# Conv inputs and the out projection's operand turned in 32 x 32 blocks on VectorE and re-partitioned through DRAM, in place of TensorE transposes

## The chip, the cores and the metric

One NeuronCore of one Trainium2 chip. The metric is the device time of one launch in microseconds (us); the kernel before takes 1271.84 us, the median of 3 runs (1271.75 to 1272.41). All numbers of the trace come from one profiled execution of the kernel before.

## The reference

Two decoder layers over x (256 tokens, 2048 channels), all float32. Each layer projects x with one wide matrix, runs three causal mixers on the result, and sends the concatenated mixer outputs through an output projection, a residual and a layer norm.

```python
(aq, ak, av, ag, su, sv, sg, mq, mk, mv, mo, mg, mi, mf) = split_columns(x @ w_in)
# A: three dilated window attentions, merged by their softmax denominators -> att
# B: sgu = u * (causal 128x128 mixing of the layer-normed v)
# C: mLSTM in chunks of 128; its q and k first pass a causal depthwise convolution of width 4
qk = silu(causal_depthwise_conv(concat(mq, mk), conv_w, conv_b))      # 2048 channels
h  = mlstm_chunkwise(q, k, v, ig, lf) * sigmoid(mo)
ml = head_norm(h, head_norm_g)
mix = concat([att * silu(ag), sgu * silu(sg), ml * silu(mg)])          # 256 x 2048
x  = layer_norm(alpha * x + mix @ w_out)
```

## The kernel before

The tokens are two tiles of 128 (`TT = 2`), the model's 2048 channels are 16 tiles of 128 (`KT`). A projection of 512 columns is a block: 8 chunks (`CH`) of 256 weight rows each. There are 23 blocks of `w_in` and 4 of `w_out` in a layer. Each float32 product is made of three passes in the fp32r type: the operand and the weights are both split into a high part and the rest (hi and lo), and hi x hi, hi x lo and lo x hi are summed in PSUM. So a chunk is 12 matmuls of 512 columns (`chunks`, L373): 2 row tiles, 2 token tiles, 3 passes.

The weights flow through a ring of four: SP issues a 512 KB load into `w_raw[c % 4]` (L324) when VectorE has finished with that slot; ScalarE copies it to `w_hi` (L736) as soon as TensorE has left the slot of `w_hi` of four chunks ago; VectorE subtracts to get `w_lo` (L1060); TensorE uses both. Everything else on ScalarE and VectorE is written between these splits in a fixed order, as is the order on SP. Each engine and each queue works strictly in its written order.

The operand of a matmul needs channels on the partitions. Where a projection's result (tokens on the partitions) becomes an operand or must be scanned along the tokens, TensorE transposes it:

- the convolution: 4 blocks of 512 columns, mq and mk (`N_CONV` to `N_CONV + 3`). Each is copied out of PSUM to `z[:, i % 2]` by ScalarE (tile 0) and VectorE (tile 1) in the next block's fourth chunk (`take`), transposed by 8 matmuls with the identity (L639, in `conv_transposes`), and then ScalarE makes bias + last tap from PSUM (L961), VectorE adds three taps, 12 instructions for 512 channels (L1404), and ScalarE applies SiLU into `qkT` (L967).
- the out projection's operand, `mix`: 8 units of 2 channel tiles, 4 transposes each (L391, in `transposes`), then the hi copy on ScalarE (L755) and the lo part on VectorE (L1084). The first two units stand inside block `N_SG`, the rest between the chunks of the first `w_out` block (`first_block`).

The blocks at the end of a layer, in the order of TensorE: `N_CONV` .. `N_CONV + 3`, `N_MV` and `N_MV + 1` (values of the mLSTM), `N_MG1` (second half of its gate), `N_SG` (gate of B), `N_OUT` .. `N_OUT + 3`. The mLSTM's score matmuls (L671) stand after the first chunks of `N_MV + 1` and wait for all of the convolution (`conv_silu`). The value matmuls (L690 to L692) stand in the block behind it. VectorE turns them into h, statistics and the normed h (`head_output`, L1462); GpSimd multiplies by the gain and by the gate (L1732, L1737). The lines of two helpers recur in the rows: L1137 and L1133 are 32 x 32 block transposes of VectorE that the attention part uses already.

## Time and profile before

| | |
|---|---|
| median of 3 runs | 1271.84 us (1271.75 to 1272.41) |
| span of the profiled execution, first to last instruction | 1269.9 us |
| TensorE busy | 1257.0 us, 99% |
| VectorE busy | 893.0 us, 70% |
| ScalarE busy | 705.4 us, 56% |
| GpSimd busy | 244.0 us, 19% |
| mean granted TensorE clock | 0.997 of full speed |
| DMA, mean | 209 GB/s, 264.97 MB |

The profiled execution's own time is not listed apart from its span; the median of the runs stands 1.9 us above the span. Matmuls overlap, so the duration of one (some 390 ns) is longer than its spacing (some 227 ns); the spacing is read from the chain of waits, where the pieces follow each other. "Idle before, releaser" says how long an engine stood still before an instruction, and whose end let it go.

### The profile page before, as it was taken

To read this page: it belongs to the slowest core of one execution; us is meant where nothing else is said; L and a number is where in the kernel's file an instruction comes from. 1 tells how busy PE (TensorE), PEld (TensorE's weight loads), DVE (VectorE), ACT (ScalarE), POOL (GpSimd) and SP (SyncE) were. 2 spreads that over 40 slices of the span, in tenths; PEclk is the share of its full clock that TensorE was granted. 3 is DMA by queue.
4 is the path that set the end of the run, shared out by engine and by line. 5 is a ranking of instruction groups with operands and counts; after the bars stand their busy time and mean duration, and the time that the engine had idled before them with its cause. 6 is when DMAs were issued, how large, how long until landed. Compare 5 with 4: busy or idle time off the path is not lost.

```text
span 1269.9 us, 16388 instructions
## 1 busy us (share of the span) xinstructions
PE 1257.0 (99%) x6342; PEld 1040.2 (82%) x6342; DVE 893.0 (70%) x1229; ACT 705.4 (56%) x989; POOL 244.0 (19%) x268
## 2 busy tenths in 40 slices
PE   9999999999999999999999999999999999999996
PEld 8888888878888888888888788888888888888885
DVE  5686876876667655865785779768665776567656
ACT  5477476575555544444563775666755555345441
POOL 0321522522220000400003223334131200004000
PEclk9999999999999999999999999999999999999998
DMA  9968768765665555465657587678546556565562
GB/s 336 310 209 261 236 189 277 260 192 164 204 195 174 184 186 185 152 230 190 207 186 238 183 282 245 193 258 282 184 149 215 183 157 209 165 197 198 186 212 86
DMA packets 129277, 264.97 MB, mean 209 GB/s; under 512 B 8824, under 2 KB 8976, under 8 KB 128688
## 3 DMA queue, kind: packets, MB, share of 16 engines
q1 hardware_dynamic: 123712, 247.23, 60.6%
q0 software_dynamic: 3680, 13.28, 3.0%
q10 hardware_dynamic: 1808, 3.42, 0.7%
q8 instruction: 50, 0.82, 0.3%
q14 instruction: 27, 0.22, 0.0%
HBM read 258.61 MB, written 5.28 MB: 208 GB/s over the span
## 4 chain that ended last, share of the span: by engine, by line
PE 86%; ACT 4%; DVE 4%; POOL 3%; issue 2%; DVEq 0%; POOLq 0%; ACTq 0%
PE ps L373 79%; ACT arena L810 2%; DVE w_lo L1060 2%; ACT w_hi L736 2%; PE ps L444 1%; PE ps L671 1%; PE ps L391 1%; PE ps L639 1%; POOL arena L1684 1%; PE ps L533 0%; POOL arena L1680 0%; PE ps L518 0%; ACT arena L807 0%; PE ps L355 0%; DVE arena L1133 0%
## 5 line engine op out<-in xcount | busy, mean ns | idle before, releaser
L1060 DVE TENSOR_TENSOR w_lo<-w_raw,w_hi 128x1024 fp32r<-128x1024 f32 x408 | 527.1, 1305 | 326.4 <-ACT w_hi L736 324.5
L736 ACT ACTIVATE w_hi<-w_raw 128x1024 fp32r<-128x1024 f32 x408 | 427.3, 1058 | 388.9 <-PE ps L373 339.3
L373 PE MATMUL ps<-w_hi,xT_hi 128*128 128x512 f32 x1616 | 636.2, 394 | 0.7 <-DVE w_lo L1060 0.7
L373 PE MATMUL ps<-w_hi,xT_lo 128*128 128x512 f32 x1616 | 629.6, 390 | 0.0
L373 PE MATMUL ps<-w_lo,xT_hi 128*128 128x512 f32 x1616 | 629.0, 389 | 0.0
L373 PEld LDWEIGHTS ps<-w_hi,xT_hi 128*128 128x128 f32 x1616 | 303.4, 188 | 64.3 <-issue 1.3
L373 PEld LDWEIGHTS ps<-w_hi,xT_lo 128*128 128x128 f32 x1616 | 303.3, 188 | 64.0
L373 PEld LDWEIGHTS ps<-w_lo,xT_hi 128*128 128x128 f32 x1616 | 303.6, 188 | 61.4
L292 POOL TENSOR_TENSOR carried<-ident 1x1 f32<-1x1 f32 x30 | 19.6, 652 | 454.8 <-DVE arena L1416 178.7
L1217 DVE CUSTOM_DVE_ANT_0 mix<-xres,mix 128x1024 f32<-128x1024 f32 x64 | 89.0, 1390 | 1.1
L807 ACT ACTIVATE arena<-arena 32x256 f32<-32x256 f32 x128 | 53.2, 416 | 15.6 <-DVE arena L1137 14.0
L373 PE MATMUL ps<-ahead,xT_hi 128*128 128x512 f32 x160 | 49.8, 392 | 0.0
L1630 POOL TENSOR_TENSOR su<-z,sincos 128x128 f32<-128x128 f32 x24 | 23.6, 1005 | 122.0 <-ACT z L796 100.9
L1404 DVE SCALAR_TENSOR_TENSOR conv_y<-ps,cw,conv_y 128x255 f32<-128x255 f32 (+2 forms) x96 | 41.7, 476 | 1.1
L1060 DVE TENSOR_TENSOR ahead<-w_raw,ahead 128x1024 fp32r<-128x1024 f32 x23 | 27.5, 1223 | 15.1 <-ACT ahead L736 15.0
L736 ACT ACTIVATE ahead<-w_raw 128x1024 fp32r<-128x1024 f32 x23 | 23.8, 1056 | 22.8 <-DMA w_raw<-w_out_dram 7.2
L373 PEld LDWEIGHTS ps<-ahead,xT_hi 128*128 128x128 f32 x160 | 29.7, 188 | 5.9
L373 PE MATMUL ps<-ahead,xT_lo 128*128 128x512 f32 x80 | 31.2, 390 | 0.0
L810 ACT ACTIVATE arena<-arena 32x256 f32<-32x256 f32 x64 | 26.6, 416 | 7.3 <-DVE arena L1133 6.5
L825 ACT ACTIVATE arena<-arena 32x256 f32<-32x256 f32 x64 | 26.6, 415 | 6.8 <-DVE arena L1165 5.9
L967 ACT ACTIVATE arena<-conv_y 128x512 f32<-128x512 f32 x16 | 10.1, 633 | 32.7 <-DVE conv_y L1404 32.7
L1732 POOL TENSOR_TENSOR store<-store,hg 128x1024 f32<-128x1024 f32 x4 | 11.4, 2876 | 76.5 <-DVE store L1462 76.5
(244 smaller groups left out, 825.3 us busy)
## 6 DMA issues: line engine op xcount, KB each, us to landing
w_raw<-w_in_dram SPq DMA_DIRECT2D x367, 512.0 KB, 4.5
w_raw<-w_out_dram SPq DMA_DIRECT2D x64, 512.0 KB, 4.8
mix<-gate_w_dram SPq DMA_DIRECT2D x32, 512.0 KB, 5.6
xres<-x_dram ACTq DMA_DIRECT2D x4, 512.0 KB, 8.4
v_dram<-arena POOLq DMA_DIRECT2D x4, 512.0 KB, 6.3
z<-v_dram POOLq DMA_DIRECT2D x8, 256.0 KB, 5.6
z<-ln_g_dram POOLq DMA_DIRECT2D x2, 1024.0 KB, 7.7
store<-ln_b_dram POOLq DMA_DIRECT2D x2, 1024.0 KB, 7.9
```

The costliest lines, as they stand in the source:

```text
L292: nc.gpsimd.tensor_tensor(carried[0:1, at:at + 1], ident[0:1, 0:1], ident[0:1, 0:1], ALU.mult)
L373: mm = pe.matmul(ps[2 * s + t][:], a[:, order[c] * KC + k, t * P:(t + 1) * P], b[:, k], start=(c + k + i == 0), stop=(c == CH - 1 and k == ...
L391: tr = pe.transpose(ps[4 + u % 4][:, (k * TT + t) * P:(k * TT + t + 1) * P], src[:, t, at * P:(at + 1) * P], ident[:])
L444: mm = pe.matmul(ps[t][:], a[:, c * KC + k, t * P:(t + 1) * P], b[:, k], start=False, stop=(c == CH - 1 and k == KC - 1 and i == 2))
L736: A(hi_of(n, c), w_raw[:, c % RING], ACT.Copy).then_inc(w_hi_done, 1)
L807: mv_ = A(dst.rearrange("p m (r t u i) -> p u t (m r) i", r=RES, t=TT, u=4)[:, u], src.rearrange("p (t f q i) -> p f t q i", t=TT, f=4, i= ...
L810: mv_ = A(dst.rearrange("p m (t u s) -> p u t m s", t=TT, u=4)[:, u], src.rearrange("p (t m f s) -> p f t m s", t=TT, m=PAIRS, f=4)[:, f], ...
L825: e = A(pTC[f * 32:(f + 1) * 32, :, u * 32:(u + 1) * 32], zp[u * 32:(u + 1) * 32].rearrange("p (s f i) -> p f s i", s=SLOTS, f=4)[:, f], A ...
L1060: TTn(lo_of(n, c), w_raw[:, c % RING], hi_of(n, c).bitcast(F32), ALU.subtract).then_inc(w_lo_done, 1)
L1217: f = V.tensor_tensor_reduce(gate_junk, xres[:, tt, half * KH:(half + 1) * KH], gate_rows[buf], 1.0, 0.0, ALU.mult, ALU.add, gate_acc[:, t ...
L1404: f = STT(y, ps[4 + hf][:, t * SEQ:(t + 1) * SEQ - back], cw[:, m, j:j + 1], y, ALU.mult, ALU.add)
L1630: G.tensor_tensor(rope_a[:, :, :, c], v[:, :, :, c], trig(1), ALU.mult)
```

## The change

Neither transposes of TensorE (L639, L391) remain; those of the attention part, the gates and the next layer's x stay.

- **Convolution.** VectorE turns the 128 x 1024 tile of a block in 32 x 32 blocks (one STREAM_TRANSPOSE). That leaves each 32-token, 32-channel square transposed in place, so channels still have to move between partition quadrants: SP stores the turned tile to DRAM (`put_conv`, one DMA, rows of 576 bytes) and reads it back in four DMAs of 32 partitions each (`fetch_conv`). A halo of 3 tokens is filled by a memset and a small copy. Bias and taps then read the SBUF tile `conv_T` where they read PSUM before.
- **Out projection's operand.** `mix` goes the same way in four parts of 512 channels (`put`, `fetch`, rows of 512 bytes): ATT, ML_A, SGU, ML_B. The hi and lo instructions are now 128 x 1024 for ATT, SGU and ML_A, and two of 128 x 512 for ML_B.
- **Order.** The last two `w_in` blocks change places (gate of B first, then the second half of the mLSTM's gate). VectorE takes over the product of gate and gained h for ML_A and ML_B; GpSimd multiplies by the gain in halves (before: all of h, then all of the gate). The loads of the final layer norm's gain and bias on GpSimd's queue move behind the store and fetch of ML_B. The weights of `w_out` are read in plain order.

The diff, cut to its core:

```diff
+                def put_conv(i):
+                    sp.wait_ge(conv_turned, l * 4 + i + 1)
+                    dst = conv_dram[l, i].rearrange("f t u j x -> (u j) (f t) x")
+                    src = conv_zT.rearrange("p f (t m) x -> p (f t) (m x)", t=TT)
+                    sp.dma_start(dst, src).then_inc(conv_put, 16)
+                def fetch_conv(i):
+                    sp.wait_ge(conv_put, (l * 4 + i + 1) * 16)
+                    ...
+                    for f in range(4):
+                        sp.dma_start(dst[f * QUARTER:(f + 1) * QUARTER], src[f]).then_inc(conv_moved, 16)
...
+                        if c == 1 and N_CONV + 2 <= n <= N_CONV + 5:
+                            fetch_conv(n - N_CONV - 2)
+                        if c == CH - 1 and N_CONV + 1 <= n <= N_CONV + 4:
+                            put_conv(n - N_CONV - 1)
...
+                load(w_in, N_MG1, (MG + 1) * BW, plain, puts={0: ATT, 6: ML_A, 7: SGU}, fetches={2: ATT})
+                load(w_out, N_OUT, 0, plain, puts={7: ML_B}, fetches={0: ML_A, 1: SGU})
+                load(w_out, N_OUT + 1, BW, plain, fetches={0: ML_B})
...
@@ TensorE @@
-                    chunks(N_CONV + i, Q_CONV + i, i % 2, 0, 2)
-                    conv_transposes(i - 1)
-                    chunks(N_CONV + i, Q_CONV + i, i % 2, 2, 6)
+                    chunks(N_CONV + i, Q_CONV + i, i % 2, 0, 6)
...
-                transposes(mix, CH, OUT_ORDER, 0, ((h_done, (l + 1) * MH), (mix_att, l + 1)))
-                transposes(mix, CH, OUT_ORDER, 1)
-                chunks(N_SG, Q_SG, 1, 4, CH)
-                first_block(N_OUT, Q_OUT, mix, CH, OUT_ORDER, 2, {
-                    2: ((h_done, (l + 1) * MH), (mix_ml, l + 1)),
-                    6: ((z_dve, taken_dve(l, Q_SG)),)})
+                chunks(N_MG1, Q_MG1, 1, 0, CH)
+                for c in range(CH):
+                    pe.wait_ge(mixT_lo, step(l, c))
+                    chunks(N_OUT, Q_OUT, 0, c, c + 1)
...
@@ ScalarE, convolution @@
-                    act.wait_ge(conv_ps, l * 4 + i + 1)
+                    split(n + 1, 0, 2)
+                    act.wait_ge(conv_moved, (l * 4 + i + 1) * 4 * 16)
...
@@ VectorE, convolution @@
+                    take(n, i % 2, z[:, i % 2, 1, :])
+                    V.transpose(conv_zT.rearrange("p f b x -> p b f x")[:, :, :, HALO:],
+                                z[:, i % 2].rearrange("p t c -> p (t c)")).then_inc(conv_turned, 1)
+                    split(n, 4, 6)
...
+                    split(n, 6, 8)
+                    split(n + 1, 0, 2)
+                    dve.wait_ge(conv_moved, (l * 4 + i + 1) * 4 * 16)
+                    V.memset(conv_T[:, 0, :, 1:HALO], 0.0)
+                    own(V.tensor_copy(conv_T[:, 1:, :, 1:HALO], conv_T[:, :-1, :, QUARTER + 1:]))
...
+                        split(n + 1, 2 + hf, 3 + hf)
...
@@ VectorE, from the normed h to the out projection @@
+                own(TTn(mix[:, :, 2 * BW:3 * BW], mix[:, :, 2 * BW:3 * BW], store[:, 1], ALU.mult))
+                turn_mix(ML_A)
+                split(N_MG1, 3, 4)
+                TTn(mix[:, :, BW:2 * BW], mix[:, :, BW:2 * BW], su[:], ALU.mult).then_inc(z_dve, 1)
+                turn_mix(SGU)
+                split(N_MG1, 4, 8)
+                operand(ATT, 0)
+                split(N_OUT, 0, 4)
+                TTn(mix[:, :, 3 * BW:4 * BW], mix[:, :, 3 * BW:4 * BW], store[:, 2], ALU.mult).then_inc(z_dve, 1)
+                turn_mix(ML_B)
+                operand(SGU, 1)
+                operand(ML_A, 2)
+                split(N_OUT, 4, 8)
+                operand(ML_B, 3, 0, KC)
+                operand(ML_B, 4, KC, KC)
```

How the change moves instructions, first on SP. This is its queue from the convolution to the end of the first layer, before: nothing but weight loads (L324).

```order
L324 DMA w_raw<-w_in_dram 128x2x512 [waits w_lo_done] x92
L324 DMA w_raw<-w_out_dram 128x2x512 [waits w_lo_done] x32
```

The same stretch of SP now (L375 is the weight load; L342 and L350 store and fetch a convolution block, L327 and L335 a part of `mix`), one of the four convolution blocks and then the parts SGU and ML_B:

```order
L342 DMA conv_dram<-arena 128x8x144 [waits conv_turned]
L375 DMA w_raw<-w_in_dram 128x2x512 [waits w_lo_done] x2
L350 DMA arena<-conv_dram 32x8x144 [waits conv_put]
L350 DMA arena<-conv_dram 32x8x144 x3
L375 DMA w_raw<-w_in_dram 128x2x512 [waits w_lo_done] x6
...
L327 DMA mix_dram<-arena 128x8x128 [waits mix_turned]
L375 DMA w_raw<-w_out_dram 128x2x512 [waits w_lo_done]
L335 DMA arena<-mix_dram 32x8x128 [waits mix_put2]
L335 DMA arena<-mix_dram 32x8x128 x3
L375 DMA w_raw<-w_out_dram 128x2x512 [waits w_lo_done]
L335 DMA arena<-mix_dram 32x8x128 [waits mix_put1]
```

Weight loads now stand behind stores that wait for VectorE, and behind fetches that wait for a store to have landed.

VectorE, the last convolution block (it runs during block `N_MV`), before: `take`, two splits, six taps, two splits, six taps, then the four splits of the block behind.

```order
L1095 COPY z<-ps 128x512 [waits w_used]
L1060 TENSOR_TENSOR w_lo<-w_raw,w_hi 128x1024 [waits w_hi_done] x2
L1404 SCALAR_TENSOR_TENSOR conv_y<-ps,cw,conv_y 128x255 [waits conv_bias]
...
L1060 TENSOR_TENSOR w_lo<-w_raw,w_hi 128x1024 [waits w_hi_done] x2
L1404 SCALAR_TENSOR_TENSOR conv_y<-ps,cw,conv_y 128x255 [waits conv_bias]
...
L1060 TENSOR_TENSOR w_lo<-w_raw,w_hi 128x1024 [waits w_hi_done] x4
L1410 MEMSET arena 128x8 [waits mix_att]
```

The same place now:

```order
L1108 COPY z<-ps3 128x512 [waits w_used]
L1402 STREAM_TRANSPOSE arena<-z 128x8x4x32 [waits z_dve,z_act]
L1073 TENSOR_TENSOR w_lo<-w_raw,w_hi 128x1024 [waits w_hi_done] x6
L1417 MEMSET arena 128x4x3 [waits conv_moved]
L1418 COPY arena<-arena 128x28x3
L1425 SCALAR_TENSOR_TENSOR conv_y<-arena,cw,conv_y 128x256 [waits conv_bias,own_dve]
...
L1073 TENSOR_TENSOR w_lo<-w_raw,w_hi 128x1024 [waits w_hi_done]
L1425 SCALAR_TENSOR_TENSOR conv_y<-arena,cw,conv_y 128x256 [waits conv_bias]
...
L1073 TENSOR_TENSOR w_lo<-w_raw,w_hi 128x1024 [waits w_hi_done]
L1432 MEMSET arena 128x8 [waits mix_att,conv_done]
```

The taps have moved behind six splits, two of them of the next block (`N_MV + 1`), in whose first chunk the scores wait for them.

VectorE from the normed h to the out projection, before (L1462 the norm, L1084 the lo part of a unit of `mix`, L1471 the product of SGU):

```order
L1462 TENSOR_SCALAR store<-store,mv,rstd 128x256 x7
L1060 TENSOR_TENSOR w_lo<-w_raw,w_hi 128x1024 [waits w_hi_done]
L1095 COPY mix<-ps 128x512 [waits w_used]
L1060 TENSOR_TENSOR w_lo<-w_raw,w_hi 128x1024 [waits w_hi_done] x4
L1084 TENSOR_TENSOR xT_lo<-ps,xT_hi 128x512 [waits xt_hi] x2
L1060 TENSOR_TENSOR w_lo<-w_raw,w_hi 128x1024 [waits w_hi_done] x4
L1084 TENSOR_TENSOR xT_lo<-ps,xT_hi 128x512 [waits xt_hi] x2
L1471 TENSOR_TENSOR mix<-mix,su 128x2x512 [waits z_act]
L1060 TENSOR_TENSOR w_lo<-w_raw,w_hi 128x1024 [waits w_hi_done]
```

And now (L1485 the norm, L1489, L1493 and L1501 the products of ML_A, SGU and ML_B, L1097 the turns, L1092 the lo parts):

```order
L1485 TENSOR_SCALAR store<-store,mv,rstd 128x256 x7
L1489 TENSOR_TENSOR mix<-mix,store 128x2x512 [waits ml_gain,h_norm]
L1097 STREAM_TRANSPOSE arena<-mix 128x8x4x32 [waits own_dve]
L1073 TENSOR_TENSOR w_lo<-w_raw,w_hi 128x1024 [waits w_hi_done]
L1493 TENSOR_TENSOR mix<-mix,su 128x2x512 [waits z_act]
L1097 STREAM_TRANSPOSE arena<-mix 128x8x4x32 [waits z_dve]
L1073 TENSOR_TENSOR w_lo<-w_raw,w_hi 128x1024 [waits w_hi_done] x4
L1092 TENSOR_TENSOR xT_lo<-z,xT_hi 128x1024 [waits mixT_hi]
L1073 TENSOR_TENSOR w_lo<-w_raw,w_hi 128x1024 [waits w_hi_done] x4
L1501 TENSOR_TENSOR mix<-mix,store 128x2x512 [waits z_act,store_gain]
L1097 STREAM_TRANSPOSE arena<-mix 128x8x4x32 [waits z_dve]
L1092 TENSOR_TENSOR xT_lo<-arena,xT_hi 128x1024 [waits mixT_hi] x2
```

Two products and two turns now stand between the norm and the splits of the last `w_in` block, and the product and turn of ML_B stand ahead of the lo parts of SGU and ML_A.

## Rows read from the trace of the kernel before

**Rows 1.** The page: span, busy time and share by engine.
```profile
span 1269.9 us, 16388 instructions
PE 1257.0 (99%) x6342; PEld 1040.2 (82%) x6342; DVE 893.0 (70%) x1229; ACT 705.4 (56%) x989; POOL 244.0 (19%) x268
```

**Rows 2.** The page, costliest groups: line, engine, operation, count, busy, mean ns, idle, releaser.
```profile
L1060 DVE TENSOR_TENSOR w_lo<-w_raw,w_hi 128x1024 fp32r<-128x1024 f32 x408 | 527.1, 1305 | 326.4 <-ACT w_hi L736 324.5
L736 ACT ACTIVATE w_hi<-w_raw 128x1024 fp32r<-128x1024 f32 x408 | 427.3, 1058 | 388.9 <-PE ps L373 339.3
```

**Rows 3.** The chain that ended last, first layer: start, length, what.
```profile
447.07 0.87 PE ps L639 x8
447.94 19.05 PE ps L373 x84
467.00 1.31 PE ps L671 x8
...
510.41 19.06 PE ps L373 x84
...
542.15 2.74 PE ps L373 x12
545.33 2.76 PE ps L373 x12
```

**Rows 4.** All groups by line: the transposes that go, taps, turns, a product.
```profile
L1404 DVE SCALAR_TENSOR_TENSOR conv_y<-ps,cw,conv_y 128x255 f32<-128x255 f32 (+2 forms) x96 | 41.7, 476 | 1.1
...
L1137 DVE STREAM_TRANSPOSE arena<-z 128x512 f32<-128x512 f32 x16 | 16.8, 1130 | 0.0
...
L391 PE MATMUL ps<-ident,mix 128*128 128x128 f32 x64 | 8.9, 272 | 0.0
L639 PE MATMUL ps<-ident,z 128*128 128x128 f32 x64 | 8.3, 272 | 0.0
...
L1133 DVE STREAM_TRANSPOSE arena<-z 128x1024 f32<-128x1024 f32 x4 | 5.0, 1238 | 2.5 <-POOL z L1634 2.5
...
L1471 DVE TENSOR_TENSOR mix<-mix,su 128x1024 f32<-128x1024 f32 x2 | 2.4, 1216 | 0.0
```

**Rows 5.** The timeline of VectorE, the last convolution block and the norm: start, length.
```profile
443.95 0.68 DVE L1095 COPY z<-ps 128x512 f32<-128x512 f32 x1
...
455.73 2.68 DVE L1404 SCALAR_TENSOR_TENSOR conv_y<-ps,cw,conv_y 128x255 f32<-128x255 f32 x6
...
518.42 2.67 DVE L1462 TENSOR_SCALAR store<-store,mv,rstd 128x256 f32<-128x256 f32 x8
521.02 1.22 DVE L1060 TENSOR_TENSOR w_lo<-w_raw,w_hi 128x1024 fp32r<-128x1024 f32 x1
...
524.48 11.30 DVE L1060 TENSOR_TENSOR w_lo<-w_raw,w_hi 128x1024 fp32r<-128x1024 f32 x4 [1.65 <-ACT w_hi L736]
```

**Rows 6.** The timeline of ScalarE: the last SiLU of the convolution.
```profile
458.44 0.63 ACT L967 ACTIVATE arena<-conv_y 128x512 f32<-128x512 f32 x1 [3.89 <-DVE conv_y L1404]
```

**Rows 7.** GpSimd: the two products at the end of the layer, and one of 128 x 512.
```profile
521.18 5.71 POOL L1732 TENSOR_TENSOR store<-store,hg 128x1024 f32<-128x1024 f32 x2 [38.26 <-DVE store L1462]
526.97 6.60 POOL L1737 TENSOR_TENSOR mix<-mix,store 128x1024 f32<-128x1024 f32 x2
...
132.70 1.04 POOL L1681 TENSOR_TENSOR arena<-arena,factor 128x512 f32<-128x512 f32 x1
```

**Rows 8.** The DMA view: SP's queue, then issues with size and us to landing.
```profile
q1 hardware_dynamic: 123712, 247.23, 60.6%
w_raw<-w_in_dram SPq DMA_DIRECT2D x367, 512.0 KB, 4.5
out_dram<-xres SPq DMA_DIRECT2D x4, 512.0 KB, 2.7
```

**Rows 9.** The weight load's line: SP's time to issue one, and time to landing.
```profile
L324 SPq DMA_DIRECT2D w_raw<-w_in_dram x367: 367/368/1133, 2.2 to 1151.0; - x184
DMA to landing us min/median/max: 3.3/4.6/8.2
```

More of the change, by code:

```diff
@@ L62 @@
 N_LOOP = 1
-N_SU, N_SV, N_CONV, N_MV, N_MG1, N_SG, N_OUT = 13, 14, 15, 19, 21, 22, 23
+N_SU, N_SV, N_CONV, N_MV, N_SG, N_MG1, N_OUT = 13, 14, 15, 19, 21, 22, 23
 NBLK = 27
-Q_GATES, Q_SU, Q_SV, Q_CONV, Q_MV, Q_MG1, Q_SG, Q_OUT = 13, 14, 15, 16, 20, 22, 23, 24
+Q_GATES, Q_SU, Q_SV, Q_CONV, Q_MV, Q_SG, Q_MG1, Q_OUT = 13, 14, 15, 16, 20, 22, 23, 24
 QBLK = 28
-OUT_ORDER = (0, 1, 4, 5, 6, 7, 2, 3)
+PARTS = 4
+PART_TILES = KT // PARTS
+ATT, SGU, ML_A, ML_B = range(PARTS)
+TURN_ORDER = (ATT, ML_A, SGU, ML_B)
+STEPS = PARTS + 1
 XP = D // BW
@@ L300, in _, with put, fetch, load @@
             for l in range(DEPTH):
-                def load(w, n, col, order, gate=()):
+                def put(p):
+                    sp.wait_ge(mix_turned, l * PARTS + TURN_ORDER.index(p) + 1)
+                    dst = mix_dram[l, p].rearrange("f t u j x -> (u j) (f t) x")
+                    sp.dma_start(dst, mix_zT[p].rearrange("p (a x) -> p a x", a=4 * TT)).then_inc(mix_put[p], 16)
+                def fetch(p):
+                    sp.wait_ge(mix_put[p], (l + 1) * 16)
+                    src = mix_dram[l, p].rearrange("f t u j x -> f j (t u) x")
+                    dst = mix_T[p].rearrange("p (b x) -> p b x", b=SEQ // QUARTER)
+                    for f in range(4):
+                        sp.dma_start(dst[f * QUARTER:(f + 1) * QUARTER], src[f]).then_inc(mix_moved[p], 16)
+                def put_conv(i):
[5 more added lines that the diff above has]
+                    sp.wait_ge(conv_put, (l * 4 + i + 1) * 16)
+                    src = conv_dram[l, i].rearrange("f t u j x -> f j (t u) x")
+                    dst = conv_T.rearrange("p b m x -> p b (m x)")
+                    for f in range(4):
+                        sp.dma_start(dst[f * QUARTER:(f + 1) * QUARTER], src[f]).then_inc(conv_moved, 16)
+                def load(w, n, col, order, gate=(), puts={}, fetches={}):
                     for c in range(CH):
@@ L378, in chunks @@
                             mm.then_inc(done, 1)
-                def transposes(src, first, order, u, ready=()):
-                    for sm, value in ready:
-                        pe.wait_ge(sm, value)
-                    if u >= 4:
-                        pe.wait_ge(xt_lo, mix_first(l) + u - 3)
-                    for k in range(KC):
-                        for t in range(TT):
-                            at = order[u] * KC + k
-                            tr = pe.transpose(ps[4 + u % 4][:, (k * TT + t) * P:(k * TT + t + 1) * P],
-                                              src[:, t, at * P:(at + 1) * P], ident[:])
-                    tr.then_inc(xt_ps, 1)
                 def unit(l, i):
@@ L446, in by_product @@
                     mm.then_inc(w_used, 1)
-                def first_block(n, q, src, first, order, u0, ready):
-                    for u in range(u0, 4):
-                        transposes(src, first, order, u, ready.get(u, ()))
-                    for c in range(CH):
-                        pe.wait_ge(xt_lo, mix_first(l) + c + 1)
-                        chunks(n, q, 0, c, c + 1, order)
-                        if c + 4 < CH:
-                            transposes(src, first, order, c + 4, ready.get(c + 4, ()))
                 if l == 0:
@@ L657, in _ @@
                     chunks(N_CONV + i, Q_CONV + i, i % 2, 6, CH)
-                chunks(N_MV, Q_MV, 0, 0, 2)
-                conv_transposes(3)
-                chunks(N_MV, Q_MV, 0, 2, CH)
+                chunks(N_MV, Q_MV, 0, 0, CH)
                 def mlstm_scores(h):
```

207 lines of the change are left out of this document (105 added, 102 removed).

## The prediction

> **What bounds the kernel now.** I read the page first. TensorE is busy 1257.0 of a span of 1269.9 us [rows 1]; the reader should see that nothing done on another engine can shorten the time unless it takes work off TensorE, and that work put on another engine is free until TensorE has to wait for it. Then the groups: VectorE and ScalarE spend most of their time on the weight splits and wait for each other and for TensorE [rows 2], so they run just behind TensorE. Then the chain of waits, which here is TensorE's own row of matmuls; its pieces give the spacing. Last the timelines of VectorE and ScalarE at the two places that the change rewrites, for the slack.
>
> A chunk takes 2.72 us: 84 matmuls, 7 chunks, in 19.05 us [rows 3]. A block of 8 is 21.8 us.
>
> **What goes.** A set of 8 transposes stands in the chain with 0.87 us [rows 3], 0.109 us each. Between 542.15 and 545.33 in the chain are a chunk of 2.74 us and one unit of four transposes, 0.44 us, the same price. There are 64 + 64 of them [rows 4]: 128 x 0.109 = 14.0 us, 7.0 in a layer. All of it is on TensorE, so all is gained if no wait comes in its place. The hi and lo copies change their source from PSUM to SBUF and their number, on engines with room; I cost that at nothing.
>
> Three places can give it back. I follow each in times relative to TensorE, with 0.05 to 0.1 us for a handoff.
>
> **1. The last convolution block against the mLSTM scores.** Before, the last taps end at 455.73 + 2.68 = 458.4 and the SiLU at 459.1 [rows 5, 6], the scores start at 467.0 [rows 3]: 8 us of slack. Now the taps stand behind the split of chunk 1 of the next block. Let `N_MV` start at 0 on TensorE. That split needs the slot of chunk 5 of `N_MV`, free at 6 x 2.72 = 16.3. ScalarE ends it at 17.4 and VectorE at 18.7 (1.06 and 1.22 us, [rows 2, 5]). The halo's memset and copy are in no row; between the 0.13 of nearly nothing and the 0.68 of a 128 x 512 copy [rows 5] I take 0.3: 19.0. Six taps 2.68 [rows 5], 21.7; a split, 22.9; six taps, 25.6; the SiLU 0.63 [rows 6], 26.3. TensorE wants the scores after 9 chunks, at 24.5. It waits 1.8 us. (Taps from SBUF may be shorter than from PSUM: the 1216 ns of a 128 x 1024 product of SBUF tiles [rows 4] is 1.19 ns an element, 0.30 for 256, against 0.45: then 0 to 1 us. They may be no faster: 1.8.) The lower end I take at 0.5.
>
> This holds if the data is there by 17.4. VectorE comes to the new turn late, since the taps of the block before end at 25.6 - 21.8 = 3.8; a split and the copy of 0.68 make 5.7. The turn of 128 x 1024 costs 1.24 if it is like L1133, and 2 x 1.13 if its strided output is like L1137 [rows 4]; its output runs are 32 elements long as in L1133, so 1.24: 6.95. A store and four fetches follow. A 512 KB DMA of SP lands 2.7 to 4.6 us after its issue [rows 8, 9]; with 4.6 for the store, and for the fetches 3 more issues of 0.37 [rows 9] and again 4.6, the data lands at 17.4. Just in time, with up to 3 us in hand if the lower figure holds. SP waits about 4 us between two weight loads for it; a load is issued when its slot's last split is done, about 2.3 us after TensorE began a chunk, and its own split of 2.3 must be done 7 chunks after that begin: 19.05 - 4.6 = 14.4 us against a median landing of 4.6, so this hides.
>
> The other three blocks have 4 us more: the taps' last split of chunk 2 is ready at 22.9, needed at 27.2. VectorE's load in such a block is 8 splits 9.8, copy 0.7, turn 1.2, halo 0.3, taps 5.4, together 17.4 of 21.8 us; it fits.
>
> **2. The block ahead of the out projection.** Let its start be 0 (before: 510.41 + 19.06 - 4 x 2.72 = 518.6, [rows 3]). Before, the norm starts at 518.42, so at -0.2, and the next splits are ready long ahead. Now the turn of ATT, 1.24, stands ahead of the four head outputs, and I give 1.0 of it through to the norm, since VectorE had almost no idle there. The norm ends at 3.5 (2.67, [rows 5]), product of ML_A 1.22, turn 1.24, split 3, product and turn of SGU, split 4: 3.5 + 2 x 1.24 + 4 x 1.22 + handoffs = 11.3. TensorE needs chunk 4 at 10.9. On top, GpSimd's gain on half of h starts when the norm ends. What such work costs VectorE shows at 524.48: four splits take 11.30 instead of 4.9 us beside L1732 and L1737 [rows 5, 7]. So 6.4 us were lost beside four GpSimd products of 128 x 1024, that is eight of 128 x 512 with 1.04 each alone [rows 7], 8.3 us: 0.77 per us. The new piece is 2 x 1.04, so 1.6. Split 4 is ready at 12.9 and TensorE waits 2.0 us. With no clash it is 0.4; with the full 2.1, 2.5.
>
> The Trainium skill (SBUF — State Buffer, "SBUF: two separate sides") says that VectorE and GpSimd hold a shared port pair for a whole instruction and the other blocks fully; a VectorE instruction takes part only with two SBUF inputs or in a two-port mode. By that rule the turns would not be held, and the loss could be one GpSimd product, 1.04 us: the term would be 1.4 for 2.0, and the time 1.2 us lower.
>
> **3. The first `w_out` block.** Let it start at 0. The split of its chunk 3 needs the slot that frees at 0: ScalarE 1.1, VectorE 2.35. ScalarE's two SiLUs of the gate come after it (about 0.6 each as L967), then VectorE's product, 3.6, the turn of ML_B, 4.9, and only then the lo part of SGU, priced like a product of 128 x 1024: 6.2. Chunk 2 wants it at 5.45: a wait of 0.8 us, at least. ML_B is turned at 5.0, stored by 9.6, fetched by 15.3 (4.6, and 1.1 + 4.6), hi 0.6 and lo 0.7 on one half: 16.8. Chunk 6 wants it at 16.35 + 0.8 = 17.1. It is hidden by 0.3 us. If the weights of chunks 2 and 3 come late, the product starts later: SP issues them behind the fetches, and a landing of 8.2 as the worst in [rows 9] would push 3 us into this place.
>
> **Sum.** Per layer 7.0 - 1.8 - 2.0 - 0.8 = 2.4 us, for two layers 4.8. The traced span would be 1269.9 - 4.8 = 1265.1. The median of the runs shown stands 1.9 us above that span, so the time is 1271.84 - 4.8 = 1267.0 us. With the small ends of the three waits (0.5, 0.4, 0.8) the gain is 5.3 a layer, 1261.2; with 1.8, 2.5 and 3.8 there is a loss of 1.1 a layer, 1274.0. That is the likeliest case's own range.
>
> **Rival A, slower: the small rows of the round trip.** The stores and fetches move 512 or 576 bytes at a time. SP's queue now moves 123712 packets of 2 KB in 60.6% of 16 x 1269.9 us [rows 8]: 99.5 ns a packet, 16 packets an engine in a 512 KB load, 1.6 us. The new transfers have 64 an engine. In proportion to the bytes one costs 25 ns, 1.6 us again; at the price of a whole 2 KB packet 6.4 us. No row shows which. Every us more per transfer comes twice in the round trip, at the last convolution block and at ML_B, in both layers. With the 0.3 us in hand at ML_B the gain is gone when a transfer costs 0.7 us more, 36 ns a packet. At 50 ns it is 1.6 us more: waits of 5.0, 2.0, 0.8 and 2.9 = 10.7 a layer, so 3.7 lost, and 1271.84 + 7.4 = 1279.2 us. At 99.5 ns the queue would also be full in each convolution block (8 loads 12.7 + 12.7 us against 21.8) and the time well over 1300. For it: the turned data crosses HBM twice in small rows, beside weight loads that hold the engines at 60% already. Against: rows of half a kilobyte are not tiny, and the four stores of 512 KB at the end land in 2.7 us.
>
> The Trainium skill has rules on both sides. DMA: Bandwidth & Descriptors, "Specifications", puts the least transfer for line rate at 512 bytes; by it the sum stands. Perfetto Trace Analysis, "DMA Optimizations", says that DMAs under 2 KB have a significant overhead per transfer; by it this rival is right. And VectorE: DVE Perf Modes, "Rules for kernel authors", advises TensorE for a 128 x 128 transpose where PSUM will do as the destination; the rows agree only so far as TensorE's 0.109 us is the cheapest of all steps here, which is why the gain can't exceed 14 us.
>
> **Rival B, no change: the order on VectorE eats it.** Terms 2 and 3 at their large ends and the late weights, without slow packets: 1.8 + 2.5 + 2.2 = 6.5 a layer, 1.0 us in all, 1270.8 us. For it: before, four splits already took 11.30 us here, and the landing of a weight load reaches 8.2 [rows 5, 9]. Against: GpSimd's work in this place shrinks from 12.3 us [rows 7] to some 2.
>
> **Rival C, the waits are hidden.** Transfers land early, taps from SBUF are fast, the turn and products slip between the splits: only 0.8 at SGU stays, and the gain is 12.4, 1259.4 us. Against: the split of chunk 1 ahead of the taps is held by TensorE itself and no faster engine moves it.
>
> **How the numbers follow.** Chances: my forecast 0.50, A 0.20, B 0.20, C 0.10. Faster or slower means by over 0.2% (2.5 us), about what a measurement of this kernel can tell from no change. Of the forecast's case 0.40 lies below 1269.3, 0.07 within, 0.03 above; C is all faster; B is 0.03 faster, 0.14 same, 0.03 slower; A 0.03 same (packets just above 36 ns), 0.17 slower. Together faster 0.53, same 0.24, slower 0.23. The range is 1261.2, the forecast's lower end, to 1278, most of the way to A's 50 ns; C beyond its lower end and A's worse half lie outside, about 0.2.
>
> **What would show it.** In the chain after: no L639 or L391; a break of TensorE ahead of the first score matmul, some 2 us, released by ScalarE's SiLU or VectorE's taps; one ahead of chunk 4 of the block before the out projection, released by the w_lo split; one ahead of chunk 2 of the first `w_out` block, released by the lo part of SGU. The store should land some 4 us after issue and the fetches 5; if either shows 6 or more, A is at work, and breaks stand also inside the four convolution blocks. If the first break is over 3 us, my landing at 17.4 was wrong. The forecast fails if TensorE's idle grows by less than 4 or more than 14 us over both layers.

## The result and the profile after: slower, 1283.6 us against 1271.8

The changed kernel took 1283.63 us (median of 4 runs, 1281.40 to 1286.79), the kernel before beside it 1271.80 us (4 runs). The ratio is 1.0094, 95% interval 1.0079 to 1.0109: slower by 11.8 us, where I forecast 4.8 us faster. The time lies above the predicted range of 1261.2 to 1278. Medians here are of all runs but one: an execution of e5 that took 3251.80 us was in a slower state and is left out.

The page of the changed kernel, as [rows 1, 8] for the one before:

```profile
span 1281.9 us, 16250 instructions
...
PE 1251.4 (98%) x6214; PEld 1031.4 (80%) x6214; DVE 906.2 (71%) x1257; ACT 705.6 (55%) x983; POOL 232.0 (18%) x266
...
q1 hardware_dynamic: 157760, 265.06, 67.5%
```

TensorE's 128 transposes are gone (6342 instructions, now 6214), but it is busy only 5.6 us less [rows 1], not 14.0, and the span is 12.0 us longer. So time was lost in two ways: TensorE waits, and it works more slowly. What it waits for (line waited for, us in total, times, longest):

```profile
PE ps L688 <- ACT arena L979: 9.1, 2, 4.8
PE ps L435 <- DVE xT_lo L1092: 7.9, 2, 4.1
...
```

Two waits in each layer and no others that matter (one of 1.6 us at the start is there before too, and the rest are 0.7 us and less): the scores of head 0 wait for the last convolution SiLU, and chunk 2 of the first `w_out` block for the lo part of SGU. How TensorE works behind a wait stands in the windows of the first layer (after the stretch: its length and busy time of each engine, then PEclk, the DMA share and GB/s):

```profile
440.00:460.00 20.00, 20.00 (x90) 16.57 (x89) 13.94 (x19) 9.86 (x13) 0.00 (x0) 1.00 0.81 232
460.00:480.00 20.00, 15.69 (x66) 12.84 (x65) 12.24 (x21) 7.70 (x11) 0.00 (x0) 0.83 0.47 144
...
469.00:472.00 3.00, 3.00 (x10) 2.52 (x10) 1.56 (x2) 0.00 (x0) 0.00 (x0) 0.50 0.77 212
554.00:558.00 4.00, 4.00 (x12) 3.14 (x11) 2.26 (x2) 0.67 (x1) 0.00 (x0) 0.57 0.53 153
```

A granted clock of 0.50 is 1.2 GHz, the lower of the two levels; 1.00, as ahead of the wait, is 2.4 GHz; figures between are stretches with some of each. The chain shows the price (start, length, what):

```profile
467.30 2.93 PE ps L688 x8
470.24 3.81 PE ps L435 x12
...
552.91 7.13 PE ps L435 x23
```

Eight score matmuls take 1.31 us at the full clock [rows 3] and 12 others 2.77: behind the first wait 1.62 + 1.04 = 2.66 us are lost. Behind the second, 23 matmuls at 19.05 / 84 = 0.227 us [rows 3] would be 5.2: 1.9 us.

The account of the first layer is then 4.3 + 2.7 + 3.9 + 1.9 = 12.8. In the second layer the scores take 2.93 us again and the 12 behind them 3.54, so 1.62 + 0.77 = 2.4, and the chain behind the second wait loses 1.9 as before: 4.8 + 2.4 + 4.1 + 1.9 = 13.2. From the 26.0 come off 14.0 for the transposes: +12.0, and the spans differ by 12.0.

**Where the first wait comes from.** The chain through the last convolution block, from the turn to the taps:

```profile
445.63 1.26 DVE arena L1402
...
446.90 3.69 DMA conv_dram<-arena
...
450.61 0.33 SPq L350
...
452.13 6.76 DMA arena<-conv_dram
...
458.92 0.03 ACT conv_y L972
```

and the timelines of ScalarE and VectorE beside it, VectorE's with the first taps of the two blocks ahead:

```profile
455.60 1.06 ACT L750 ACTIVATE w_hi<-w_raw 128x1024 fp32r<-128x1024 f32 x1 [1.23 <-DMA w_raw<-w_in_dram]
458.92 2.09 ACT L972 ACTIVATE conv_y<-arena,cb,cw 128x256 f32<-128x256 f32 x4 [2.26 <-DMA arena<-conv_dram]
```
```profile
414.04 2.72 DVE L1425 SCALAR_TENSOR_TENSOR conv_y<-arena,cw,conv_y 128x256 f32<-128x256 f32 x6 [0.18 <-ACT conv_y L972]
...
437.31 2.72 DVE L1425 SCALAR_TENSOR_TENSOR conv_y<-arena,cw,conv_y 128x256 f32<-128x256 f32 x6 [0.99 <-ACT conv_y L972]
...
456.69 1.23 DVE L1073 TENSOR_TENSOR w_lo<-w_raw,w_hi 128x1024 fp32r<-128x1024 f32 x1 [1.06 <-ACT w_hi L750]
458.94 0.19 DVE L1418 COPY arena<-arena 128x84 f32<-128x84 f32 x1 [1.02 <-issue]
460.11 2.71 DVE L1425 SCALAR_TENSOR_TENSOR conv_y<-arena,cw,conv_y 128x256 f32<-128x256 f32 x6 [0.99 <-ACT conv_y L972]
```

The block starts at 438.3 on TensorE. The data lands at 458.9, which is 20.6 into it, where I had 17.4. Three things are late ahead of the taps: the split of chunk 1 ends 0.9 us later than I had it, since its own weights landed late; the data lands 1.0 us after that split; and the 0.99 us of ScalarE's first two bias products, which I had hidden behind the splits, now stand between landing and taps. The halo copy, 0.19 us, runs beside these products and costs nothing, where I had 0.3. So the scores start 29.0 into the block for my 26.3: 2.7 us later, of which 2.5 show as wait (4.3 for 1.8).

Where the 3.2 us of the landing come from the same rows tell: the turn ends at 446.9, 8.6 into the block, 1.6 later than my 6.95; the store is 0.9 quicker than my 4.6 (3.69); the last fetch is issued 1.5 after the store's landing for my 1.1; it takes 6.8, 2.2 more than my 4.6. (That is 3.3; my sum had 0.1 of handoffs in it.) The turn is late because the lateness is handed on from block to block. A block takes 21.8 us on TensorE, but the first taps start at 414.04, 437.31 and 460.11, 23.3 and 22.8 us apart: taps, turn, store, fetches and the next taps form a chain that is longer than a block.

**Where the second comes from.** The chain ahead of chunk 2 of the first `w_out` block:

```profile
532.81 0.70 SPq L335
...
537.28 0.45 SPq L335
...
537.77 0.45 SPq L375
...
538.27 8.72 DMA w_raw<-w_out_dram
...
547.01 1.07 ACT w_hi L750
...
548.10 1.00 DVE w_lo L1073
...
549.25 1.23 DVE mix L1501
...
550.50 1.25 DVE arena L1097
551.75 1.12 DVE xT_lo L1092
```

Chunk 3's weights are issued behind eight fetches and land after 8.7 us; the split, the last part's product and turn, and the SGU operand follow in one row. Between 540 and 553 the DMA share is 0.96.

### The profile page after: what moved, and what is told of

It is laid out like the page before. It is cut to its first block, busy times and chain, and to the rows that moved or that the text cites. A ratio compares the mean times of both kernels' runs of the same rounds, so it can differ in the third digit from the quotient of the medians.

```text
span 1281.9 us, 16250 instructions
## 1 busy us (share of the span) xinstructions
PE 1251.4 (98%) x6214; PEld 1031.4 (80%) x6214; DVE 906.2 (71%) x1257; ACT 705.6 (55%) x983; POOL 232.0 (18%) x266
## 3 DMA queue, kind: packets, MB, share of 16 engines
q1 hardware_dynamic: 157760, 265.06, 67.5%
## 4 chain that ended last, share of the span: by engine, by line
PE 69%; DVE 12%; DMA 7%; ACT 5%; issue 3%; SPq 2%; POOL 2%; DVEq 0%; ACTq 0%; POOLq 0%
PE ps L435 63%; DVE w_lo L1073 5%; DMA arena<-conv_dram 3%; DVE conv_y L1425 3%; ACT w_hi L750 2%; PE ps L491 2%; DMA w_raw<-w_in_dram 1%; DMA conv_dram<-arena 1%; DMA w_raw<-w_out_dram 1%; PE ps L688 1%; DVE mix L1230 1%; ACT arena L820 1%; SPq L350 1%; SPq L335 1%; DVE arena L1402 1%
## 5 line engine op out<-in xcount | busy, mean ns | idle before, releaser
L1073 DVE TENSOR_TENSOR w_lo<-w_raw,w_hi 128x1024 fp32r<-128x1024 f32 x408 | 515.7, 1277 | 315.4 <-ACT w_hi L750 313.2
L817 ACT ACTIVATE arena<-arena 32x256 f32<-32x256 f32 x128 | 53.2, 416 | 17.4 <-DVE arena L1150 15.8
L1425 DVE SCALAR_TENSOR_TENSOR conv_y<-arena,cw,conv_y 128x256 f32<-128x256 f32 x96 | 42.2, 481 | 6.2 <-ACT conv_y L972 5.0
L1771 POOL TENSOR_TENSOR store<-store,hg 128x512 f32<-128x512 f32 x4 | 7.2, 1821 | 198.3 <-DVE store L1485 198.3
L750 ACT ACTIVATE ahead<-w_raw 128x1024 fp32r<-128x1024 f32 x23 | 23.8, 1056 | 22.8 <-DMA w_raw<-w_in_dram 7.9
L688 PE MATMUL ps<-arena 128*128 128x256 f32 (+1 forms) x64 | 14.7, 382 | 9.1 <-ACT arena L979 9.1
```

The source lines that it names most:

```text
L688: mm = pe.matmul(ps[4 + h % 2][:, cols], qkT[:, 8 + 2 * h + d, s * P:(s + 1) * P], qkT[:, 2 * h + d, t0:SEQ], start=(d == 0), stop=(d == 1))
L750: A(hi_of(n, c), w_raw[:, c % RING], ACT.Copy).then_inc(w_hi_done, 1)
L817: mv_ = A(dst.rearrange("p m (r t u i) -> p u t (m r) i", r=RES, t=TT, u=4)[:, u], src.rearrange("p (t f q i) -> p f t q i", t=TT, f=4, i= ...
L1073: TTn(lo_of(n, c), w_raw[:, c % RING], hi_of(n, c).bitcast(F32), ALU.subtract).then_inc(w_lo_done, 1)
L1425: f = STT(y, conv_T[:, :, 2 * hf + t, HALO - back:HALO - back + QUARTER], cw[:, m, j:j + 1], y, ALU.mult, ALU.add)
```

## Experiments

The theory to be tested: these two waits, with the low clock behind each, are the whole loss. Rivals: short rows load the DMA engines everywhere; the order of the issuing queue or of the two elementwise engines is at fault; the low clock is not due to the waits. The kernel before, run beside each group, had medians of 1271.91, 1271.62 and 1271.75 us.

**e1, the conv half alone.** Before, with the new convolution on all engines:

```
-                chunks(N_CONV + i, Q_CONV + i, i % 2, 0, 2)
-                conv_transposes(i - 1)
-                chunks(N_CONV + i, Q_CONV + i, i % 2, 2, 6)
+                chunks(N_CONV + i, Q_CONV + i, i % 2, 0, 6)
```

> The kernel before with the conv half of the change alone: the conv inputs are turned on VectorE and re-partitioned through DRAM, while the out projection's operand is transposed on TensorE as before. Theory T (the loss is two TensorE waits per layer, each followed by matmuls at the lower of the two granted clocks; here only the first of them, ahead of the scores of head 0): 32 of the 64 transposes of a layer are gone, -7.0 us over both layers; 2 x (4.5 of wait + 2.65 of slow matmuls) = +14.3; sum +7.3, 1279.1 us, and the page shows one wait of PE on ACT arena of 4 to 5 us, twice. Rival R (the small packets slow all weight loads, wherever they stand): conv moves 8 of 16 MB-like round trips, so about half of the loss, +6, but spread over many short waits. Rival O (order on VectorE, not the transfer): same total, but the taps wait for VectorE, not for DMA.

Measured 1275.66 us, ratio 1.0031 (1.0021 to 1.0041): +3.8.

**e2, the out projection's half alone.**

```
-                first_block(N_OUT, Q_OUT, mix, CH, OUT_ORDER, 2, {...})
+                for c in range(CH):
+                    pe.wait_ge(mixT_lo, step(l, c))
+                    chunks(N_OUT, Q_OUT, 0, c, c + 1)
```

> The kernel before with the out projection's half of the change alone (the order of the two last blocks ahead of it swapped, turns of mix on VectorE, four parts through DRAM), the conv inputs transposed on TensorE as before. Theory T: -7.0 us of transposes, + 2 x (4.0 of wait ahead of chunk 2 of the first w_out block + 1.9 of slow matmuls) = +11.8; sum +4.8, 1276.6 us; the scores start without a wait. Rival R: about +6 in many short waits. If the two halves hurt each other through shared transfers, e1 and e2 together come to less than the +11.8 of the full change; by theory T they add up to +12.1.

Measured 1278.55 us, ratio 1.0056 (1.0043 to 1.0069): +6.6. TensorE's waits in the two, e1 first:

```profile
PE ps L694 <- ACT arena L992: 8.2, 2, 5.0
```
```profile
PE ps L428 <- DVE xT_lo L1103: 9.8, 2, 5.1
```

Each half brings its own wait and nothing else, and the halves add up to 10.4 of the 11.8 us. My split between them was off: 7.3 and 4.8 expected. In e1 the wait of the first layer is 3.2 us with PEclk 0.91 over 460 to 480, so it costs less; in e2 the waits are 4.7 and 5.1. The halves together lose no more than the whole, within the 1.4 us that are missing, so each wait needs the other half of the change for next to nothing. Rival R fails: no short waits are spread over either page. Rival O fails for e1, since in its chain too the last taps wait for the landing (457.7), not for VectorE.

**e3, the scores two chunks later.**

```
+                chunks(N_MV + 1, Q_MV + 1, 1, 0, 2)
                 for h in range(MH):
-                    chunks(N_MV + 1, Q_MV + 1, 1, h, h + 1)
+                    chunks(N_MV + 1, Q_MV + 1, 1, h + 2, h + 3)
                     mlstm_scores(h)
-                chunks(N_MV + 1, Q_MV + 1, 1, MH, CH)
+                chunks(N_MV + 1, Q_MV + 1, 1, MH + 2, CH)
```

> The changed kernel with TensorE doing chunks 0, 1 and 2 of the second mLSTM value block ahead of the scores of head 0, instead of chunk 0 alone: 5.5 us of matmuls that have to be done anyway fill the wait. Nothing on any other engine is changed. Theory T: the wait of 4.5 us and the slow stretch behind it (2.65) go, in both layers: -14.3, 1269.3 us; the granted clock of the stretch 460 to 480 goes from 0.83 to 1.00. Rival 1 (the wait is only handed on: VectorE takes the scores later and the attention of mLSTM is late in the next block): the wait of 3 to 4 us turns up at the first numerator matmuls, time within 2 us of 1283.6. Rival 2 (the lower clock comes from something else than the idle time, such as the score matmuls themselves): -9.0, 1274.6, and the scores still take 2.9 us.

Measured 1271.48 us, ratio 1.0001 (0.9992 to 1.0010): 12.1 us faster than the changed kernel (14.3 expected; the spans differ by 13.4), by moving nothing but TensorE's own matmuls. Its chain has no break there:

```profile
454.95 13.83 PE ps L435 x61
468.78 1.31 PE ps L688 x8
470.08 2.77 PE ps L435 x12
```

The granted clock of 460 to 480 is 1.00. Rival 1 fails (no new wait, only the one at `w_out` is left, 8.5 us); rival 2 fails (the scores take 1.31 us).

**e4, matmuls that do nothing in the waits.**

```
+                    if h == 0:
+                        filler(18)      # ps[7] <- xT_hi, 512 columns, read by nobody
                     mlstm_scores(h)
```

and `filler(16)` ahead of chunk 2 of the first `w_out` block. Since the filler writes `ps[7]`, TensorE also waits for `sgu_done` ahead of the block with the scores and for `h_done` ahead of the first `w_out` block; no wait shows at either.

> The changed kernel with 18 matmuls of 512 columns (4.1 us at the full clock) whose result nobody reads put ahead of the scores of head 0, and 16 (3.7 us) ahead of chunk 2 of the first w_out block, so that TensorE works through both waits. The waits themselves stay: the scores can't start earlier. Theory T: only the slow stretches go, 2 x (2.65 + 1.9) = -9.1, 1274.5 us, and the score matmuls of head 0 take 1.3 us instead of 2.9. Rival 2 (the lower clock has another cause): no gain, 1283 to 1285, and the scores still take 2.9 us. If the fillers overshoot the waits, some tenths of a us per place are lost.

Measured 1277.10 us, ratio 1.0036 (1.0024 to 1.0049): 6.5 us less than the changed kernel, with more work in it.

```profile
463.35 4.24 PE L695 MATMUL ps<-xT_hi 128*128 128x512 f32 x18
467.44 1.57 PE L688 MATMUL ps<-arena 128*128 128x256 f32 x8
```
```profile
460.00:480.00 20.00, 20.00 (x96) 16.63 (x95) 13.16 (x22) 7.84 (x11) 0.00 (x0) 1.00 0.53 159
540.00:560.00 20.00, 19.13 (x84) 15.51 (x84) 13.02 (x11) 10.06 (x11) 0.00 (x0) 1.00 0.91 257
```

The scores start at 467.4, as in the changed kernel (467.3): the wait is the same. What is gone is the low clock. So the clock's fall is due to the idle TensorE, and it costs some 7 of the 11.8 us (span 7.9 less, median 6.5, 9.1 expected). The Trainium skill (TensorE: Matmul & The Clock Gate, "HAM oscillation — how this bites in real kernels") describes this for another kernel, a wait for data that brings the clock down for the work behind it; the rows here agree.

**e5, weights ahead of the SGU fetch on SyncE's queue.**

```
-    load(w_out, N_OUT, 0, plain, puts={7: ML_B}, fetches={0: ML_A, 1: SGU})
+    load(w_out, N_OUT, 0, plain, puts={7: ML_B}, fetches={0: ML_A, 3: SGU})
```

> The changed kernel with one thing moved on SyncE's queue: the four fetches of the SGU part are issued behind the loads of chunks 2 and 3 of the first w_out block instead of ahead of them, so that these two loads go out about 2 us earlier. Theory S (the late chunks 2 and 3 come from the place in the queue): chunk 3 lands near 545 instead of 547.0, the SiLUs, the product, the turn and the SGU operand behind it on ScalarE and VectorE come 2 us earlier, the wait of chunk 2 falls from 4.0 to about 2 us, total -4 to -6 us with part of the slow stretch, 1278 to 1280. Rival B (the 16 DMA engines are full there, and whatever is put first the rest is late): the wait goes from the weights to the SGU part and stays 3.5 us or more, time within 1.5 us of 1283.6.

Measured 1279.54 us (3 runs, 1278.14 to 1282.78), ratio 1.0067 (1.0052 to 1.0081): 4.1 us less than the changed kernel by the medians, within a scatter of 4.6 us in e5 itself. The waits at this place fall from 7.9 to 5.1 us. In the profiled run, the fastest, those at the scores are also shorter, 7.5 for 9.1 us, which this edit doesn't touch. Chunk 3's weights reach ScalarE at 543.4, not 547.0, but then ScalarE waits for the SGU part until 545.9. So theory S holds for 2.8 of the 7.9 us; for the rest the transfers themselves are late.

**e6, the order on ScalarE and VectorE.** SGU's operand ahead of the last part's SiLUs, product and turn, and chunk 3's split behind them:

```
-                split(N_OUT, 0, 4)
+                split(N_OUT, 0, 3)
+                operand(SGU, 1)
                 ...
                 turn_mix(ML_B)
-                operand(SGU, 1)
+                split(N_OUT, 3, 4)
                 operand(ML_A, 2)
```

> The changed kernel with the order on ScalarE and VectorE changed in the first w_out block, SyncE's queue as it is: the split of chunk 3 comes behind the SGU operand, the SiLUs, the product and the turn of the last part, and the SGU operand comes ahead of these. The waiting chunk 2 then needs chunk 2's weights (landed 545.6) and the SGU operand, not chunk 3's weights nor the last part's product and turn. Theory E (the wait is the order of these two engines): chunk 2 can start at about 549.0 to 549.5, the wait falls from 4.0 to 0 to 1 us and the slow stretch goes; but chunk 3 (its weights landed at 547.0, split behind the turn) may be a little late. Total 2 x (3.5 + 1.9) = -10.8, 1273 us. Rival B (late weights are what counts): the wait only moves to chunk 3, gain under 3 us.

Measured 1288.81 us, ratio 1.0136 (1.0122 to 1.0151): 5.2 us slower than the changed kernel. Theory E was wrong in the sum, though the wait at chunk 2 went as it said. The first layer's waits in this block:

```profile
549.24 0.50 PE L435 MATMUL ps<-w_hi,xT_hi 128*128 128x512 f32 x1 [0.48 <-DVE xT_lo L1093]
552.85 0.47 PE L435 MATMUL ps<-w_hi,xT_hi 128*128 128x512 f32 x1 [0.59 <-DVE w_lo L1074]
564.47 0.54 PE L435 MATMUL ps<-w_hi,xT_hi 128*128 128x512 f32 x1 [3.22 <-DVE xT_lo L1093]
```

The last row is chunk 6: the last part, stored only at 553.1 behind a load that waits for chunk 3's split, is now the late one. In the changed kernel ScalarE gets it at 563.1 as well, and the wait at chunk 2 hid that.

**e7, e6 with SyncE's queue in the order of need**, and **e8, e7 with e3.**

```
+    load(w_out, N_OUT, 0, plain, puts={6: ML_B}, fetches={3: SGU, 4: ML_A})
```

> The order of e6 together with SyncE's queue in the order of need: the loads of chunks 0 to 3 first, then the SGU fetches, the load of chunk 4, the fetches of the first mLSTM part, and the last part's store ahead of the load of chunk 7. Theory E+S: no wait left in the first w_out block, -11.8: 1272 us. Rival B: the DMA engines are near 90% in 525 to 560, the SGU part lands only after 549 and chunk 2 waits for it 1 to 3 us: 1276 to 1280.

> e7 with TensorE's order of e3 (chunks 0 to 2 of the second value block ahead of the scores of head 0): both waits of the changed kernel filled or removed. Theory T: before minus the 14.0 us of the transposes plus what waits are left (0 to 2 us): 1258 to 1260 us. Rival (a new wait comes behind: the last mLSTM part, at chunk 6 of the first w_out block, or the first numerator matmuls): 2 to 5 us back in each layer, 1262 to 1268.

e7: 1283.51 us, ratio 1.0094 (1.0079 to 1.0109), the same as the changed kernel. e8: 1272.42 us, ratio 1.0003 (0.9991 to 1.0014), the same as e3. Both lie outside what either theory or rival had forecast (1272 or 1276 to 1280; 1258 to 1260 or 1262 to 1268). The wait at chunk 2 is 0.3 us in e7, but waits of 5.5 and 3.9 us stand ahead of chunk 6 now, in e8 of 3.1 and 4.4. The chain behind the one of 5.5:

```profile
537.16 8.60 DMA arena<-mix_dram
...
545.78 1.07 ACT xT_hi L766
...
548.01 1.23 DVE mix L1503
...
555.83 8.38 DMA arena<-mix_dram
```

The last SGU fetch lands 8.6 us after its issue. The product and turn of the last part stand behind SGU's operand on VectorE, so they wait for this landing, and the last part's own fetches then take 8.4 us. A written order carries one late landing on to the next part.

**e9, long rows in the fetches.**

```
-    mix_dram (DEPTH, PARTS, 4, TT, 4, QUARTER, P)      one store, rows of 512 B; 4 fetches, rows of 512 B
+    mix_dram (DEPTH, PARTS, QUARTER, 4, TT, 4, P)      4 stores, rows of 512 B; 4 fetches, rows of 4 KB
```

and conv_dram in the same way.

> The changed kernel with the DRAM scratch laid out so that a fetch reads and writes one row of 4 KB (mix) or 4.6 KB (conv) per partition instead of eight rows of 512 or 576 B; the store keeps its short rows and becomes four DMAs of 32 partitions instead of one, which costs SyncE about 1.4 us of issuing per part. Bytes are the same, half of the short rows are gone. Rival A (the load of short rows on the 16 DMA engines makes the fetches and the weights behind them late): the DMA share of 440 to 460 falls from 0.81 to about 0.73 and that of 540 to 560 from 0.87, fetches land in about 4 us instead of 5, each of the two waits shrinks by 1 to 2 us, total -4 to -8: 1276 to 1280. Theory L (latency of two DMAs in a row and SyncE's queue set the wait, the row length does not): within 2 us of 1283.6, or 2 us more for the additional issues.

Measured 1282.32 us, ratio 1.0082 (1.0068 to 1.0095): 1.3 us less than the changed kernel. Its waits and its queue:

```profile
PE ps L438 <- DVE xT_lo L1095: 10.0, 2, 5.1
PE ps L691 <- ACT arena L982: 5.5, 2, 3.4
```
```profile
q1 hardware_dynamic: 144192, 265.07, 67.3%
arena<-conv_dram SPq DMA_DIRECT2D x32, 144.0 KB, 4.6
```

13568 packets fewer, and the share of DMA time falls by 0.2 points only: over a span of 1281 us on 16 engines about 55 us (the shares are rounded, so 35 to 75), 4 ns for each packet saved. Runs with the same packets scatter more than that, from 67.3% (e6) to 67.8% (e7), so this is no saving that can be told from none. The row length of the fetches is not what the engines' time goes to; the stores keep their short rows in every run, so for them it is untested. The time is within the scatter of the changed kernel, as theory L said. In its parts some of rival A's signs did show: the DMA share of 440 to 460 is 0.75 for 0.81, and the waits at the scores fall by 3.6 us (conv fetches land in 4.6, not 5.1; where the convolution is as in the changed kernel, in e5 to e7, these waits are 7.5 to 8.8). Those at `w_out` rise by 2.1; why was not isolated (SyncE issues three DMAs more per part).

**e10, the parts in the order in which they come ready.** With e3, and in the first `w_out` block:

```
+FIRST_ORDER = (0, 1, 4, 5, 2, 3, 6, 7)     # attention, first mLSTM part, SGU, last part
+    load(w_out, N_OUT, 0, FIRST_ORDER, puts={5: ML_B}, fetches={1: ML_A, 4: SGU, 7: ML_B})
     (VectorE:)
-                split(N_OUT, 0, 4)
+                split(N_OUT, 0, 2)
+                operand(ML_A, 1)
                 ... product and turn of ML_B
-                operand(SGU, 1)
-                operand(ML_A, 2)
+                split(N_OUT, 2, 4)
+                operand(SGU, 2)
```

> The changed kernel with the scores behind chunks 0 to 2, as in e3, and the first w_out block in the order in which its parts come ready: chunks of the attention, then of the first mLSTM part (turned 5.7 us ahead of the SGU part), then SGU, then the last part; fetches behind the loads of chunks 1, 4 and 7; the SiLUs, the product and the turn of the last part ahead of the splits of chunks 2 and 3. Chunk 2 then wants data turned at 526.6 (in the timeline of the changed kernel), not at 531.3. Theory T with D (what is late in e7 is the SGU part's round trip through full DMA engines): no wait at chunk 2, a wait of 0 to 1 us at chunk 6; 1258 to 1262 us. Rival W (the weights of chunks 2 and 3 are late by themselves, whatever is fetched when): 1.5 to 3 us of wait per layer stay, 1264 to 1268.

**e11, e10 with the rows of e9.**

> e10 with the scratch layout of e9 (rows of 4 KB in the fetches). Rival A: 1 to 4 us less than e10. Theory L: within 1 us of e10, or up to 2 us more for the additional issues on SyncE.

e10: 1260.58 us, ratio 0.9916 (0.9902 to 0.9930). e11: 1260.74 us, ratio 0.9915 (0.9901 to 0.9928). Both beat both kernels: 11.2 us less than before, of 14.0 possible. The waits of e10:

```profile
PE ps L436 <- DVE xT_lo L1095: 2.6, 2, 1.5
...
PE ps L436 <- DVE w_lo L1076: 1.5, 2, 0.8
```

In its windows PEclk is 1.00 in 460 to 480 and in 540 to 560, behind its waits of up to 1.5 us too. The DMA share of 540 to 560 is 1.08 (the view's figure), higher than in the changed kernel: here full engines did little harm once what they carried was asked for in the order in which it was needed. The largest wait of e10 stands at chunk 6. The product of the last part starts there at 538.2, 15.1 us ahead of the end of chunk 5's matmuls; in e7 it was 12.2 (548.0 and 560.2). The time is that of theory T with D, and rival W's weight waits of 1.5 to 3 us a layer are not there (0.8 us at most). Against e8 the edit changes only the first `w_out` block, and is worth 11.8 us; which of its parts (TensorE's order, the queue, the two engines) gives how much was not taken apart. Long rows in the fetches bring nothing a second time.

## Why the prediction was wrong

Two terms of the sum were too small and one cost had no term. The waits at the last convolution block and at the first `w_out` block were 4.3 to 4.8 and 3.9 to 4.1 us a layer for my 1.8 and 0.8, and the low clock behind them, which the sum put at nothing, cost 4.3 to 4.6 us a layer.

**The gain** was right: 64 transposes a layer and 0.109 us each. The account above closes with 14.0 us.

**Term 1, the last convolution block,** had the right place and the wrong size: 1.8 us, measured 4.3 and 4.8. "Just in time" at 17.4 was the weak step. I took the chain of transfers by median landings of the kernel before, though the new traffic raises them: in 370 to 460 the DMA share is 0.83, where it was 0.59, and the last fetch alone took 6.8 us for my 4.6. And I took each block by itself, with the taps of the block before ending at 3.8 and the other three blocks at ease. They are not: each passes its lateness on, and the last turn ends 1.6 us late before any fetch has started. Both put the bias products on the path.

**Term 2, the block ahead of the out projection,** is 0, not 2.0. The turn of ATT was absorbed whole; the norm starts at 521.40, 0.2 ahead of the block's start at 521.6, exactly as before [rows 5]. GpSimd's clash is there, 1.1 us:

```profile
521.40 2.67 DVE L1485 TENSOR_SCALAR store<-store,mv,rstd 128x256 f32<-128x256 f32 x8
...
526.54 2.31 DVE L1073 TENSOR_TENSOR w_lo<-w_raw,w_hi 128x1024 fp32r<-128x1024 f32 x1
```

Split 4 is ready at 532.4, 10.8 into the block, and wanted at 10.9. The value lies below my lower end of 0.4. The 1.04 us that I had worked out by the Trainium skill's rule (SBUF — State Buffer, "SBUF: two separate sides") is nearer to the 1.1 than my 1.6.

**Term 3, the first `w_out` block,** was 0.8 at least and 3.8 if chunks 2 and 3 land late behind the fetches; measured 3.9 and 4.1. The upper end and its reason were right (chunk 3's load took 8.7 us), and I took the lower end for the sum.

**What had no term** was the clock: 2.7 and 1.9 us behind the waits of the first layer, 2.4 and 1.9 in the second, 8.9 in all; by e4 6.5 to 7.9. Without it the waits as measured (17.0 in all) would have left +3.0 us. The kernel before has no such row, since its TensorE hardly ever stops.

**The rivals.** A had the sign and nearly the size (1279.2). It priced a short packet at 36 ns and up for the gain to be gone; if all of the engine time that was added (1531 us) is that of the 34048 added packets, one took 45 ns. Yet e9 shows that this is not a price of the fetches' short rows: taking away 13568 of them gave back about 4 ns each, within the scatter. Its own sign was absent too, the stores land 3.6 and 3.9 us after their issue and the fetches 5.1 and 5.0 at the median, and no breaks stand inside the convolution blocks. What is true of A is that more traffic in the engines goes with later landings; ScalarE waited for loads of `w_out` for 28.9 us, where it was 17.6. B named late weights, which did happen, and gave them 2.2 us. C's number is reached by e10 (1260.6 against 1259.4), but by another order, not by early landings. Of my three terms only term 2 was too large; the shortfall of terms 1 and 3 and the clock outweigh it by far.

My criteria were met: the first break is over 3 us, which I had said would prove the landing at 17.4 wrong, and TensorE's idle (span less busy) grew by 17.6 us, more than the 14 at which the forecast was to fail.

Open: how the landing of 6.8 us divides into bytes, other loads ahead of it and latency; no run changed one of these alone. Also open is why the added traffic costs the engines 86 ns a KB against 50 before, and whether the stores' short rows have a part in it.

## What to carry to other kernels

Price a wait of the bounding engine at its length plus the slow work behind it; here waits of 4 to 5 us cost 6 to 7. When work moves from the bounding engine into DMA round trips, do not size them by the landings of the old trace, and order consumers by when their data comes ready: the same change was 11.8 us slower or 11.2 us faster than the kernel before, by order alone (TensorE's, the queue's and that of the two engines). When a round trip repeats, compare the length of its loop with the pace of the bounding engine: here it was 23 us against 21.8, and each block started later than the one before. An order that fixes one wait has to be followed to the next one, as e6 shows.
